# First layers: the convolution's norm in four steps among mLSTM's, K's slabs ahead of the Fourier slabs, and the fills placed anew

## The chip, the core and the metric
One of the cores of a Trainium2 chip runs the whole program. The metric is device microseconds of one execution, the median of several. The five engines run their own instruction streams, in order, and wait for each other on semaphores: PE (TensorE, matrix products into eight PSUM banks), DVE (VectorE), ACT (ScalarE), POOL (GpSimd) and SP (SyncE, here the queue that issues the weight DMAs).

## The reference, cut to what matters
Two blocks run one after the other on 512 tokens of width 1024 (and 256 context tokens in the first block). The first block has two layers. Each does, with modulation vectors that come from `silu(c) @ w_ada` (called ada here):

```
h   = modulate(rmsnorm(x), shift, scale)
z   = h @ w_in                                   # q k v o gates | fourier u | conv a, gate
ym  = mlstm(q, k, v, gates) * sigmoid(o)         # two directions, chunked, q and k through a 3-tap conv
yf  = real(fft over tokens and over 64 channels of u)
yv  = silu(layernorm(dwconv31(a * sigmoid(gate))))
x   = x + gate1 * rmsnorm(concat(ym, yf, yv) @ w_out)
x   = x + gate2 * rmsnorm(relu(modulate(rmsnorm(x)) @ w_mlp1)**2 @ w_mlp2)
```

Layer 0 does this for tokens and context, layer 1 for tokens (its context goes into mLSTM's state only). The second block has two layers with retention, sparse attention and gated linear attention. The change touches it through the shared planner alone.

## The kernel before
A planner in Python (class `Order`) writes one list of steps, and each engine's program walks that list in order and issues what it has to do for each step. So the list's order is the order of every queue. Steps are `mm` (products of a piece), `ev` (the evacuation of its bank), `post` (small products after it), `split` (ScalarE rounds a weight slab to fp32r in WHI, L2164, POOL subtracts to get the rest in RGR, L2575), and named stages: `modSplit`, `conv` (DVE, taps of the 31-tap convolution, L1673), `mPrep` (five steps that prepare mLSTM's gates), mA, mB, mC, mD, mN, mO (mLSTM), `mxSplit`.

Weights stream in the order in which the planner names them, in slabs of up to 512 KB, through a ring of six (`RING = 6`): SP issues slab i when the last product of slab i - 6 is done (L914 to L922), in order. A piece of kind F multiplies a slab of 128 columns with 512 or 256 tokens: three fp32r products for each k (L1011 to L1013). `place` (L398) decides after all else where each unit's `split` step goes: as early as ring and WHI allow, with costs in microseconds.

Side work is woven in: `begin(steps, period)` opens a list, and each `weave(us)` gives it credit that pays for steps. `run` weaves while it issues a piece and then calls `filling`, which adds a piece's time to `credit`; when this reaches `period` the next ada of `fills` goes in (`fill`, `filling`, `ada`). An ada is two slabs of 512 KB, 16 narrow products (L960), a row copy on ScalarE (L2230), four small products (L1141, L1142) and one small addition on DVE (L1514). `rest(side)` issues what is left of mLSTM's list with one ada after every second step, and `filled` issues the adas that then remain, one behind the other.

`first_layer` (L508) goes: norm and eight modSplits; the conv's `cu` products, the first two side by side (`abreast`); gates; `glu`; `u`; the end of mPrep; the Fourier stage, dftA (L1064) and dftB (L1079) for each token region, with slabs dftc and dfts; then K, v, Q and og products; then the convolution's layernorm (lnA, L1088/L1089, sums and squares; lnB, L1094/L1095, then on ScalarE a Sqrt, on DVE a reciprocal L1685 and two multiplications L1689, on ScalarE Silu L2292); then the mxSplits, the rest of mLSTM and the `w_out` products. `ahead` names the slabs of the first two tasks before other steps; until now it serves the first products alone. PE waits with a piece until the earlier content of its PSUM bank is evacuated; these products turn over the banks 0, 1, 6 and 7.

Of the kernel before, what the change touches and what calls it, by code (L numbers as in the profile page):

```python
# [143 lines left out]
class Order:  # L144
# [54 lines left out]
    def run(self, n, parts, us):  # L199

        for part in parts:
            self.step("mm", n, part)
            self.early()
            self.weave(us / len(parts))
        for m in self.after:
            self.step("post", m)
        self.after = []
        self.step("ev", n)
        self.filling(us)
# [128 lines left out]
    def products(self, jobs, banks=(0, 1), together=0):  # L338
# [54 lines left out]
    def place(self):  # L393
# [114 lines left out]
def first_layer(o, l):  # L508
# [10 lines left out]
    cu = [F(2320, 256, "cu", "evacV", go)]  # L519
    if l == 0:  # L520
        cu = o.ahead(cu)
        o.step("gains", l, (0,))
    else:
        o.laid = [(1, j, "w_ada", 1) for j in range(44, 48, 2)]
        o.step("gains", l, (0,))
        cu = o.norms("o0b", tag, cu)
# [5 lines left out]
    else:  # L532
        o.fill(10.0, (2, range(0, 24, 2), "ada_w_2", 0), (3, range(8, 20, 2), "ada_w_2", 1))
    o.products(cu, (0, 1, 6, 7), 2)
    o.gates(l, tag, (0, 1, 6, 7))
    prep = o.begin([("mPrep", l, i) for i in range(5)], 5.0, -6.0)
    o.products([F(2576, 256, "glu", "evacA", go)], (0, 1, 6, 7))
    conv = o.begin([("conv", l, j, t0, tn, k0) for j in range(2) for t0, tn, _ in oregs for k0 in range(0, 31, 4)], 3.6 if l == 0 else 5.0)
    o.products([F(2064, 256, "u", None, go)], (0, 1, 6, 7))
    o.end(prep)  # L540
    for t0, tn, _ in oregs:
        n = tn // 128
        for ti in range(n):
            for j in range(2):
# [12 lines left out]
    o.products([F(512, 512, "qk", "evacV", GB, dst="K"), T(1024, 512, "v", None, at=[[2, 3, 4], [5, 2, 3]]), F(0, 512, "qk", "evacV", go, dst="Q")],  # L557
               (0, 1, 6, 7))
# [94 lines left out]
def schedule():  # L653
# [7 lines left out]
    o.adas(0, (8,), "w_ada", 0)  # L661
    o.step("rstd", "x0a")
    o.adas(0, (10, 12, 14), "w_ada", 0)
    o.flush()
    for l in range(2):
        first_layer(o, l)
# [39 lines left out]
def design(nc, dram):  # L706
# [779 lines left out]
    def vector(e):  # L1486
# [174 lines left out]
        def conv(l, j, t0, tn, k0):  # L1661
# [4 lines left out]
            for k in range(k0, min(31, k0 + 4)):  # L1666
# [14 lines left out]
        def lnB(p, n):  # L1681
            l, t0, tn = p["l"], p["t0"], p["tn"]
            rs = LNRS[:, 0:tn]
            e.wait_ge(*at("evacA", n))
            e.reciprocal(rs, rs).then_inc(*up("evacV"))  # L1685
            e.wait_ge(*now("evacV"))
            for i in range(2):
                x = MX[:, 6 + i, t0:t0 + tn]
                e.scalar_tensor_tensor(out=x, in0=x, scalar=vec("g_conv_ln", l)[:, i:i + 1], in1=rs, op0=MUL, op1=MUL).then_inc(  # L1689
                    *up("evacV", ("ln", l, i, t0)))  # L1690
# [61 lines left out]
        evacs = {"cu": cu, "glu": glu, "qk": qk, "v": v, "u": u, "ab": ab, "four": four, "lnA": lnA, "lnB": lnB, "out": out,  # L1752
# [368 lines left out]
        def gNorm(l, h):  # L2121
# [7 lines left out]
                  "position": position, "table": table, "ret": ret, "rSq": rSq, "rRoot": rRoot, "rNorm": rNorm, "idx": idx, "top": top, "head": head, "gSums": gSums,  # L2129
# [5 lines left out]
    def scalar(e):  # L2135
# [149 lines left out]
        def lnB(p, n):  # L2285
            l, t0, tn = p["l"], p["t0"], p["tn"]
            e.wait_ge(*at("matmuls", n))
            e.activation(LNRS[:, 0:tn], bank(p), ACT.Sqrt, scale=1.0 / 256, bias=eps).then_inc(*up("evacA", n))
            for i in range(2):
                x = MX[:, 6 + i, t0:t0 + tn]  # L2290
                e.wait_ge(*at("evacV", ("ln", l, i, t0)))
                e.activation(x, x, ACT.Silu, bias=vec("b_conv_ln", l)[:, i:i + 1]).then_inc(*up("evacA", ("conv out", l, i, t0)))  # L2292
# [267 lines left out]
        stages = {"start": start, "split": split, "xsum": xsum, "rstd": rstd, "residual": residual, "modSplit": modSplit, "ev": ev, "post": post,  # L2560
# [163 lines left out]
```

## Time and profile before
| | |
|---|---|
| three runs | 3358.75, 3350.33, 3354.8 us, median 3354.8 |
| profiled execution | 3353.06 us, span 3351.3 us |
| PE busy | 3051.1 us, 91% |
| DVE, ACT, POOL busy | 1417.9, 1009.1, 1046.3 us |
| weight slabs | 504 DMAs of 512 KB, 3.5 us from issue to landing |

The profiled execution is one run with its instructions recorded, and its span runs from the first to the last of them; all positions below are microseconds from that start. Layer 0's mixer lies from about 44 to 560, layer 1's from about 1176 to 1580. Busy time of PE says that a product was in flight. The granted clock (PEclk) is a mean over a stretch: 1.00 is 2.4 GHz, 0.50 is 1.2 GHz. A wait is put down to the instruction that ended it.

### The profile page before, as it was taken

What the parts mean: (1) busy time and instruction counts of PE and PEld (TensorE: products, weight loads), DVE (VectorE), ACT (ScalarE), POOL (GpSimd) and SP (SyncE); (2) the same over time, 40 slices, a digit from 0 to 9 for tenths busy, and PEclk for the clock granted to TensorE, in tenths of its full rate; (3) what the DMA queues carried; (4) which work ended last, traced back from release to release, by engine and by line L of the source; (5) the groups of instructions that cost most, each with busy time, mean ns of one, the idle gap of its engine ahead of it and who ended that gap; (6) DMA issues with size and microseconds to landing.
All of it is one profiled execution on the core that took longest, in us unless ns stands there. A gap on an engine that the chain in (4) does not pass through costs nothing.

```text
span 3351.3 us, 41178 instructions
## 1 busy us (share of the span) xinstructions
PE 3051.1 (91%) x16748; PEld 2452.1 (73%) x16748; DVE 1417.9 (42%) x2601; ACT 1009.1 (30%) x1640; POOL 1046.3 (31%) x508
## 2 busy tenths in 40 slices
PE   6899779899999979967999998999889989998898
PEld 4688568788888857756777776777667767776676
DVE  4584442513324256243521134644472246534822
ACT  3213432312213231333332232233423322334232
POOL 1121114222222412214244442232245423332455
PEclk9999878999999889978899989999999889999999
DMA  5332341111111123321222222122112222121121
GB/s 201 120 113 106 114 164 58 57 63 64 63 63 63 53 82 113 120 95 63 92 94 95 92 67 80 60 69 65 60 56 78 77 70 70 63 64 63 57 70 69
DMA packets 77708, 275.39 MB, mean 82 GB/s; under 512 B 8512, under 2 KB 10304, under 8 KB 77392
## 3 DMA queue, kind: packets, MB, share of 16 engines
q1 hardware_dynamic: 75824, 268.91, 23.8%
q10 hardware_dynamic: 1696, 3.84, 0.3%
q8 instruction: 134, 2.20, 0.3%
q14 instruction: 54, 0.44, 0.0%
HBM read 270.62 MB, written 2.10 MB: 81 GB/s over the span
## 4 chain that ended last, share of the span: by engine, by line
PE 78%; DVE 12%; ACT 4%; issue 3%; POOL 2%; DMA 1%; SPq 0%; DVEq 0%; ACTq 0%; POOLq 0%
PE pb L1011 19%; PE pb L1013 18%; PE pb L1012 18%; PE pb L1121 2%; PE pb L1033 2%; PE pb L1035 2%; PE pb L1034 2%; PE pb L960 2%; POOL RGR L2575 1%; PE pb L1051 1%; PE pb L1052 1%; PE pb L1053 1%; PE pb L1079 1%; DMA RG<-in_W_dram 1%; DVE AR L2071 1%
## 5 line engine op out<-in xcount | busy, mean ns | idle before, releaser
L2575 POOL TENSOR_TENSOR RGR<-RG,WHI 128x1024 fp32r<-128x1024 f32 x354 | 864.4, 2442 | 1861.0 <-ACT WHI L2164 1860.7
L2164 ACT ACTIVATE WHI<-RG 128x1024 fp32r<-128x1024 f32 x354 | 370.5, 1047 | 387.0 <-PE pb L1013 288.3
L1011 PE MATMUL pb<-HI,WHI 128*128 128x512 f32 (+1 forms) x880 | 376.9, 428 | 25.1 <-POOL RGR L2575 7.8
L1013 PE MATMUL pb<-LO,WHI 128*128 128x512 f32 (+1 forms) x880 | 354.5, 403 | 0.0
L1012 PE MATMUL pb<-HI,RGR 128*128 128x512 f32 (+1 forms) x880 | 354.4, 403 | 0.0
L1011 PE MATMUL pb<-HR,WHI 128*128 128x512 f32 (+1 forms) x768 | 278.9, 363 | 16.8 <-POOL RGR L2575 10.1
L1013 PE MATMUL pb<-HR,WHI 128*128 128x512 f32 (+1 forms) x768 | 277.7, 362 | 0.0
L1012 PE MATMUL pb<-HR,RGR 128*128 128x512 f32 (+1 forms) x768 | 277.5, 361 | 0.0
L1013 PE MATMUL pb<-HIDR,WHI 128*128 128x512 f32 (+1 forms) x768 | 274.8, 358 | 0.0
L1011 PE MATMUL pb<-HIDR,WHI 128*128 128x512 f32 (+1 forms) x768 | 273.8, 356 | 1.1 <-ACT RLT L2310 0.8
L1012 PE MATMUL pb<-HIDR,RGR 128*128 128x512 f32 (+1 forms) x768 | 274.2, 357 | 0.0
L1011 PEld LDWEIGHTS pb<-HI,WHI 128*128 128x128 f32 (+1 forms) x880 | 168.4, 191 | 93.2 <-issue 42.0
L1706 DVE TENSOR_TENSOR RLT<-RLT 128x256 f32<-128x256 f32 (+1 forms) x96 | 117.5, 1224 | 206.5 <-ACT RLT L2310 206.3
L1013 PEld LDWEIGHTS pb<-LO,WHI 128*128 128x128 f32 (+1 forms) x880 | 167.8, 191 | 44.5 <-issue 1.6
L1011 PE MATMUL pb<-HH,WHI 128*128 128x512 f32 (+1 forms) x464 | 173.2, 373 | 29.7 <-POOL RGR L2575 18.9
L1012 PEld LDWEIGHTS pb<-HI,RGR 128*128 128x128 f32 (+1 forms) x880 | 168.4, 191 | 39.2 <-issue 5.4
L1011 PEld LDWEIGHTS pb<-HR,WHI 128*128 128x128 f32 x768 | 146.9, 191 | 47.2 <-issue 24.3
L1012 PE MATMUL pb<-HH,RGR 128*128 128x512 f32 (+1 forms) x464 | 166.1, 358 | 0.0
L1013 PE MATMUL pb<-HL,WHI 128*128 128x512 f32 (+1 forms) x464 | 166.1, 358 | 0.0
L1013 PEld LDWEIGHTS pb<-HR,WHI 128*128 128x128 f32 x768 | 147.0, 191 | 23.0
L1012 PEld LDWEIGHTS pb<-HR,RGR 128*128 128x128 f32 x768 | 147.1, 191 | 22.5
L1011 PEld LDWEIGHTS pb<-HIDR,WHI 128*128 128x128 f32 x768 | 144.2, 188 | 26.4 <-issue 2.5
(407 smaller groups left out, 5622.3 us busy)
## 6 DMA issues: line engine op xcount, KB each, us to landing
RG<-in_W_dram SPq DMA_DIRECT2D x504, 512.0 KB, 3.5
XCX<-in_xT_dram ACTq DMA_DIRECT2D x4, 512.0 KB, 12.2
out_dram<-XCX SPq DMA_DIRECT2D x8, 256.0 KB, 2.1
CS<-in_CST_dram ACTq DMA_DIRECT2D x1, 1027.0 KB, 4.9
XCC<-in_ctxT_dram SPq DMA_DIRECT2D x4, 256.0 KB, 13.9
CS<-in_CST_dram SPq DMA_DIRECT2D x1, 523.0 KB, 4.8
RG<-in_W_dram SPq DMA_DIRECT2D x2, 256.0 KB, 2.9
RG<-in_W_dram SPq DMA_DIRECT2D x2, 128.0 KB, 3.4
```

The costliest lines, as they stand in the source:

```text
L960: i = e.matmul(PB[p["banks"][0]][32 * g:32 * g + 32, 0:256], CV[:, :, 4 * h + g], wt[:, g, :], start=h == 0, stop=h == 1, tile_position=(0 ...
L1011: e.matmul(out, hi[:, k, :], xh, start=k == order[0], stop=False)
L1012: e.matmul(out, lo[:, k, :], xh, start=False, stop=False)
L1013: i = e.matmul(out, hi[:, k, :], xl, start=False, stop=k == order[7])
L1033: e.matmul(out, xh[:, sl], hi[:, k, :], start=h == 0 and i0 % per == 0 and k == 0, stop=False)
L1034: e.matmul(out, xh[:, sl], lo[:, k, :], start=False, stop=False)
L1035: i = e.matmul(out, xl[:, sl], hi[:, k, :], start=False, stop=p["final"] and ends and k == nk - 1)
L1051: e.matmul(out, hi[:, k, :], xh, start=k == 0, stop=False)
L1121: m = e.matmul(sum_at(tag, c), squares_at(tag, i)[:, a:a + 128], ones[:, 0:1], start=k == 0 and c == first, stop=k == 7 and c == 5)
L1706: e.tensor_tensor(r, r, r, MUL).then_inc(*up("evacV", ("hidden", i)))
L2164: e.activation(WHI[:, u % 2, 0:n], RG[:, s % RING, 0:n], ACT.Copy).then_inc(*up("weightsA", u))
L2575: e.tensor_tensor(RGR[:, s % RING, 0:n], RG[:, s % RING, 0:n], WHI[:, u % 2, 0:n].bitcast(F32), SUB).then_inc(*up("weightsG", u))
```

## The change
The norm's last part leaves the evacuation of lnB and becomes four steps `lnOut`: two half reciprocals, then one multiplication each, the fourth with both Silus. mLSTM steps are woven between lnA and lnB and ahead of each lnOut. The convolution goes in steps of two taps with a pace by width. K's first two slabs are named before the dft slabs of the tokens (`ahead`), the preparation of the gates is taken out of the weaving during the Fourier stage and put back after it, and the credit for fills is set so that none falls into dftB and the next comes later. The period of layer 1's fills is 24 in place of 10. `rest` spreads the adas by their number. The first products' slabs come before the last two adas of the start, and `place` no longer moves a split past a modSplit. `run` issues posts earlier where more than one waits.

```diff
@@ class Order
+            while len(self.after) > 1:
+                self.step("post", self.after.pop(0))
             self.weave(us / len(parts))
@@ def rest(self, side)
+        every = max(1.5, len(side["steps"]) / max(1, len(self.fills)))
+        due = every
         for i, what in enumerate(side["steps"]):
             self.step(*what)
-            if i % 2 and self.fills:
+            if i + 1 >= due and self.fills:
+                due += every
@@ def products(self, jobs, banks, together, abreast=True)
-            if i < together:
+            if i < together and not abreast:
+                made = max(made, together)
+            elif i < together:
@@ def place(self)
-                while at + 1 < first[u] and begin[at + 1] < begin[free + 1] + 5.5 and begin[at + 1] < begin[first[u]] - 3.6:
+                while at + 1 < first[u] and begin[at + 1] < begin[free + 1] + 5.5 and begin[at + 1] < begin[first[u]] - 3.6 and self.steps[
+                        at + 1][0] != "modSplit":
@@ def first_layer(o, l, cu)
-        o.fill(10.0, (2, range(0, 24, 2), "ada_w_2", 0), (3, range(8, 20, 2), "ada_w_2", 1))
+        o.fill(24.0, (2, range(0, 24, 2), "ada_w_2", 0), (3, range(8, 20, 2), "ada_w_2", 1))
...
-    conv = o.begin([("conv", l, j, t0, tn, k0) for j in range(2) for t0, tn, _ in oregs for k0 in range(0, 31, 4)], 3.6 if l == 0 else 5.0)
+    paces = [2.4 if tn == 512 else 1.3 for j in range(2) for t0, tn, _ in oregs for k0 in range(0, 31, 2)]
+    conv = o.begin([("conv", l, j, t0, tn, k0) for j in range(2) for t0, tn, _ in oregs for k0 in range(0, 31, 2)], paces)
     o.products([F(2064, 256, "u", None, go)], (0, 1, 6, 7))
-    o.end(prep)
+    keys = None
+    o.beside.remove(prep)
...
+        if t0 == NC:
+            keys = o.ahead([F(512, 512, "qk", "evacV", GB, dst="K")])
+            o.credit = -1.0e6
...
-    o.products([F(512, 512, "qk", "evacV", GB, dst="K"), T(1024, 512, "v", None, at=[[2, 3, 4], [5, 2, 3]]), F(0, 512, "qk", "evacV", go, dst="Q")],
-               (0, 1, 6, 7))
+    o.credit = -17.0
+    o.beside.append(prep)
+    o.products(keys, (0, 1, 6, 7), 2, False)
+    o.end(prep)
+    o.products([T(1024, 512, "v", None, at=[[2, 3, 4], [5, 2, 3]]), F(0, 512, "qk", "evacV", go, dst="Q")], (0, 1, 6, 7))
...
     for t0, tn, _ in oregs:
         o.run(o.piece("lnA", [], [o.bank()], ["evacV"], l=l, t0=t0, tn=tn, how="lnA"), [ALL8], 1.7)
+        o.weave(3.0)
         o.run(o.piece("lnB", [], [o.bank()], ["evacA"], l=l, t0=t0, tn=tn, how="lnB"), [ALL8], 1.7)
+        for i in range(4):
+            o.weave(1.5)
+            o.step("lnOut", l, t0, tn, i)
+    o.weave(1.5)
@@ def schedule()
-    o.adas(0, (8,), "w_ada", 0)
+    o.adas(0, (8, 10), "w_ada", 0)
     o.step("rstd", "x0a")
-    o.adas(0, (10, 12, 14), "w_ada", 0)
+    cu = o.ahead(first_products(0))
+    o.adas(0, (12, 14), "w_ada", 0)
@@ vector
-        def lnB(p, n):
...
+        def lnOut(l, t0, tn, i):
+            h = tn // 2
+            if i == 0:
+                e.wait_ge(*at("evacA", ("ln root", l, t0)))
+            if i < 2:
+                rs = LNRS[:, i * h:i * h + h]
+                e.reciprocal(rs, rs).then_inc(*up("convV", ("ln factors", l, t0, i)))
+                return
+            x = MX[:, 4 + i, t0:t0 + tn]
+            for k in range(2):
+                e.wait_ge(*at("convV", ("ln factors", l, t0, k)))
+            e.scalar_tensor_tensor(out=x, in0=x, scalar=vec("g_conv_ln", l)[:, i - 2:i - 1], in1=LNRS[:, 0:tn], op0=MUL, op1=MUL).then_inc(
+                *up("evacV", ("ln", l, i - 2, t0)))
@@ scalar
+        def lnOut(l, t0, tn, i):
+            if i == 3:
+                for i in range(2):
+                    x = MX[:, 6 + i, t0:t0 + tn]
+                    e.wait_ge(*at("evacV", ("ln", l, i, t0)))
+                    e.activation(x, x, ACT.Silu, bias=vec("b_conv_ln", l)[:, i:i + 1]).then_inc(*up("evacA", ("conv out", l, i, t0)))
```

## Rows read from the trace of the kernel before

**Rows 1.** The page: the span, and PE's busy time (share of the span) and instructions.
```profile
span 3351.3 us, 41178 instructions
PE 3051.1 (91%) x16748; PEld 2452.1 (73%) x16748; DVE 1417.9 (42%) x2601; ACT 1009.1 (30%) x1640; POOL 1046.3 (31%) x508
```

**Rows 2.** Busy time by stretch: PE, PEld, DVE, ACT, POOL, granted clock, DMA share, GB/s.
```profile
155.00:161.00 6.00, 6.00 (x29) 5.92 (x29) 0.16 (x1) 0.20 (x1) 0.00 (x0) 0.54 0.33 135
161.00:177.00 16.00, 10.97 (x65) 8.35 (x64) 15.27 (x16) 3.71 (x6) 5.23 (x2) 0.91 0.10 33
177.00:262.00 85.00, 85.00 (x636) 75.41 (x635) 70.41 (x101) 16.77 (x26) 20.18 (x8) 1.00 0.36 124
...
357.00:393.00 36.00, 18.69 (x79) 12.80 (x80) 15.44 (x31) 13.77 (x25) 1.85 (x2) 0.66 0.14 53
...
426.00:479.00 53.00, 36.55 (x265) 27.59 (x267) 26.17 (x113) 20.09 (x45) 3.45 (x3) 0.73 0.40 146
479.00:489.00 10.00, 9.23 (x65) 5.40 (x58) 1.73 (x9) 3.67 (x6) 4.71 (x4) 0.50 0.70 244
1240.00:1249.00 9.00, 1.10 (x3) 0.89 (x4) 8.07 (x33) 0.51 (x2) 0.00 (x0) 0.64 0.34 130
...
1277.00:1318.00 41.00, 40.93 (x255) 35.18 (x254) 32.60 (x45) 10.28 (x15) 9.79 (x5) 0.96 0.24 83
1318.00:1430.00 112.00, 107.95 (x759) 91.60 (x758) 38.75 (x72) 28.83 (x46) 26.59 (x11) 1.00 0.40 137
1426.00:1451.00 25.00, 16.90 (x104) 12.00 (x103) 10.41 (x18) 12.02 (x23) 2.06 (x2) 0.93 0.36 132
...
1477.00:1529.00 52.00, 24.45 (x132) 21.95 (x130) 26.16 (x108) 17.65 (x37) 3.67 (x3) 0.71 0.04 17
```

**Rows 3.** Timeline, layer 0's first modSplits: start, us, engine, line, operation, [idle before <-releaser].
```profile
46.42 1.14 DVE L1601 SCALAR_TENSOR_TENSOR HL<-AR,MOD,HH 128x256 fp32r<-128x256 f32 x2
...
48.36 4.87 POOL L2575 TENSOR_TENSOR RGR<-RG,WHI 128x1024 fp32r<-128x1024 f32 x2 [47.91 <-ACT WHI L2164]
...
48.78 4.99 DVE L1601 SCALAR_TENSOR_TENSOR HL<-AR,MOD,HH 128x256 fp32r<-128x256 f32 x2
...
50.92 0.55 PE L1011 MATMUL pb<-HH,WHI 128*128 128x256 f32 x1 [7.50 <-POOL RGR L2575]
```

**Rows 4.** Chain of waits behind dftB, layer 0, then layer 1: start, us, what.
```profile
147.21 3.53 DMA RG<-in_W_dram
...
151.96 2.35 POOL RGR L2575
...
1268.83 3.94 DMA RG<-in_W_dram
```

**Rows 5.** Chain between layer 1's u and dftA.
```profile
1241.72 0.60 DVE AR L1650
...
1248.27 5.90 PE pb L1064 x16
```

**Rows 6.** Chain at K's evacuations, layer 0: a tap beside POOL, and one alone.
```profile
163.00 2.79 DVE AR L1673
...
166.60 0.76 DVE AR L1673
```

**Rows 7.** Timeline, the norm of layer 0.
```profile
386.47 3.35 DVE L1685 RECIPROCAL AR<-AR 128x512 f32<-128x512 f32 x1 [2.70 <-ACT AR L2288]
...
392.37 2.07 PE L1234 MATMUL pb<-CS 64*128 64x128 f32 x8 [7.81 <-DVE AR L1878]
```

**Rows 8.** Chain, an ada in a full stretch and what follows it.
```profile
409.50 1.03 PE pb L960 x16
...
411.07 1.00 PE pb L1255 x8
```

**Rows 9.** Timeline of ACT, a table load and the activation behind it.
```profile
355.12 1.28 ACT L2277 ACT_TABLE_LOAD   x1
356.42 0.60 ACT L2277 ACTIVATE AR<-pb 128x512 f32<-128x512 f32 x1
```

More of the change, by code:

```diff
@@ L336, in gates, with products @@
         self.after.append(p)
-    def products(self, jobs, banks=(0, 1), together=0):
+    def products(self, jobs, banks=(0, 1), together=0, abreast=True):
         tasks = jobs if together else self.tasks(jobs)
@@ L505, in norm_stages, with first_products, first_layer @@
     return [(x + "Sq", l, h) for h in range(5)] + [(x + "Root", l)] + [(x + "Norm", l, h) for h in range(4)]
-def first_layer(o, l):
+def first_products(l):
+    return [("F", "w_in", l, 0, 2320, 256, "cu", "evacV", {"groups": GB if l == 0 else GX, "x": "H1", "tag": f"x{l}a"})]
+def first_layer(o, l, cu):
     go = GB if l == 0 else GX
@@ L517, in T @@
         return ("T", "w_in", l, 0, c0, n, how, by, {"tiles": range(6), "x": "H1", "tag": tag, **more})
-    cu = [F(2320, 256, "cu", "evacV", go)]
     if l == 0:
-        cu = o.ahead(cu)
         o.step("gains", l, (0,))
@@ L525, in first_layer @@
         o.step("gains", l, (0,))
-        cu = o.norms("o0b", tag, cu)
+        cu = o.norms("o0b", tag, first_products(l))
     for k in range(8):
@@ L660, in schedule @@
     o.step("xsums")
-    o.adas(0, (8,), "w_ada", 0)
+    o.adas(0, (8, 10), "w_ada", 0)
     o.step("rstd", "x0a")
-    o.adas(0, (10, 12, 14), "w_ada", 0)
+    cu = o.ahead(first_products(0))
+    o.adas(0, (12, 14), "w_ada", 0)
     o.flush()
     for l in range(2):
-        first_layer(o, l)
+        first_layer(o, l, cu)
     for l in range(2):
@@ L1665, in conv @@
                 e.wait_ge(*at("evacV", ("glu", o.last["glu", l, "evacA", None])))
-            for k in range(k0, min(31, k0 + 4)):
+            for k in range(k0, min(31, k0 + 2)):
                 f = off31[t0] - 15 + k
@@ L1679, in lnA @@
                 e.scalar_tensor_tensor(out=x, in0=bank(p), scalar=-1.0 / 256, in1=x, op0=MUL, op1=ADD).then_inc(*up("evacV", n))
-        def lnB(p, n):
[L1682 to L1690, printed above, removed]
+        def lnOut(l, t0, tn, i):
[11 more added lines that the diff above has]
+                *up("evacV", ("ln", l, i - 2, t0)))
         def out(p, n):
@@ L1750, in gateY @@
                 e.tensor_tensor(y, y, SGT[j], ADD).then_inc(*up("evacV", ("sum", l, n2, j)))
-        evacs = {"cu": cu, "glu": glu, "qk": qk, "v": v, "u": u, "ab": ab, "four": four, "lnA": lnA, "lnB": lnB, "out": out,
+        evacs = {"cu": cu, "glu": glu, "qk": qk, "v": v, "u": u, "ab": ab, "four": four, "lnA": lnA, "out": out,
                  "out2": out2, "relu2": relu2, "plus": plus, "v2": v2, "cp": cp, "silu2": silu2, "gateY": gateY}
@@ L2128, in vector @@
                   "modSplit": modSplit, "pads": pads, "conv": conv, "mPrep": mPrep, "mA": mA, "mB": mB, "mC": mC, "mD": mD, "mN": mN, "mO": mO,
-                  "position": position, "table": table, "ret": ret, "rSq": rSq, "rRoot": rRoot, "rNorm": rNorm, "idx": idx, "top": top, "head": head, "gSums": gSums,
+                  "lnOut": lnOut, "position": position, "table": table, "ret": ret, "rSq": rSq, "rRoot": rRoot, "rNorm": rNorm, "idx": idx, "top": top, "head": head, "gSums": gSums,
                   "gStart": gStart, "gLevel": gLevel, "gOut": gOut, "gState": gState, "gSq": gSq, "gRoot": gRoot, "gNorm": gNorm}
@@ L2287, in lnB @@
             e.wait_ge(*at("matmuls", n))
[L2288 to L2292, printed above, removed]
+            e.activation(LNRS[:, 0:tn], bank(p), ACT.Sqrt, scale=1.0 / 256, bias=eps).then_inc(*up("evacA", n, ("ln root", l, t0)))
+        def lnOut(l, t0, tn, i):
[4 more added lines that the diff above has]
+                    e.activation(x, x, ACT.Silu, bias=vec("b_conv_ln", l)[:, i:i + 1]).then_inc(*up("evacA", ("conv out", l, i, t0)))
         def out(p, n):
@@ L2558, in gRoot @@
             e.activation(GRS, PB[3][:, 384:400], ACT.Sqrt, scale=1.0 / 128, bias=eps).then_inc(*up("glaA", ("root", l)))
-        stages = {"start": start, "split": split, "xsum": xsum, "rstd": rstd, "residual": residual, "modSplit": modSplit, "ev": ev, "post": post,
+        stages = {"lnOut": lnOut, "start": start, "split": split, "xsum": xsum, "rstd": rstd, "residual": residual, "modSplit": modSplit, "ev": ev, "post": post,
                   "mPrep": mPrep, "mA": mA, "mB": mB, "mN": mN, "mO": mO, "mxSplit": mxSplit, "position": position, "table": table, "ret": ret, "rSq": rSq,
```

## The prediction, before the result
> **What bounds the kernel now.** I read the page first: TensorE is busy for 91% of a span of 3351.3 us [rows 1], and the chain that ends last is mostly TensorE. Nothing is to be won inside its products; what an edit of order can win is the remaining 300 us of idle time, the half-rate time behind each pause, and work that can move from a full stretch into a pause. Then the table by stage [rows 2]: in it PE busy against the length of the stretch is what to see. The projections run full (177 to 262: 85.0 of 85), and beside them stand pauses: 5.0 us in 161 to 177, 17.3 in 357 to 393 (the convolution's norm of layer 0), 16.5 in 426 to 479 (mLSTM), 7.9 in 1240 to 1249, 8.1 in 1426 to 1451 (the norm of layer 1) and 27.6 in 1477 to 1529 (mLSTM). Last I took the chain of waits in each pause, to see who ends it [rows 3 to 7].
>
> **The start.** The two weight splits of the first products are issued behind the second modSplit. POOL does both from 48.36 to 53.23, and VectorE's two operations that begin at 48.78 take 4.99 us where the pair before them took 1.14; the first product starts at 50.92 behind POOL [rows 3]. After the change these slabs are loaded ahead of the last two adas, and no split is moved past a modSplit, so both splits run before VectorE begins its modSplits. VectorE gets back 3.85 us; ScalarE now does two splits (1.2 each at most, the gap between the DMA's end and POOL's start in [rows 4]) ahead of the last ada's row copy, of which some 0.7 puts off the gains. Net 3 us (bounds: 0, if the slabs land late, and 5). VectorE and PE are nearly level in the eight modSplits, so not more. The Trainium skill (SBUF — State Buffer, section "SBUF: two separate sides") says that a VectorE operation with two SBUF inputs and a GpSimd operation that reads SBUF take one shared port as an exclusive lock. By that rule the trace agrees, and it would be blocked for at most one POOL split, 2.4 us, each time the two meet. That speaks against the change in one place: K's first two splits now meet the convolution's taps in the Fourier stage instead of an idle VectorE.
>
> **K's slabs before the Fourier slabs.** K's first slab needs ring places that the four dft slabs hold until their last product. The chain shows it: DMA from 147.21, split, POOL until 154.31, 7.1 us; in layer 1 from 1268.83, DMA 3.94, then the same ScalarE and POOL work (3.5), 7.4 us [rows 4]. With both slabs ahead of dft's and split during it, PE goes straight on: 7.1 + 7.4 = 14.5 us. What is late next: the four dft slabs then hang on the last u products and one ada, and their stage begins some 6 us of small products later, so they land in time; K's third slab hangs on K's first task, 8.4 us ahead of use against the 7.1 of the same path. Bounds 10 and 14.5. Behind each pause PE runs at the low level: 155 to 161 is granted 0.54 [rows 2], and six microseconds at half rate do three microseconds' work. That is 2 to 3 us in both layers each, and 1.7 in layer 1's small products after 1248. Of some 6 I take 4 (bounds 0 and 6).
>
> **Gates' preparation.** In layer 1 its steps 3 and 4 stand between u and the Fourier products. VectorE ends u's copy at 1242.32 and PE starts dftA at 1248.27 [rows 5]: 5.95 us. The copy itself stands behind four taps of the convolution; with two taps a step it comes 1.5 us sooner. 7.4 off. The steps now fall into K's first pieces. PE reaches step 4 some 5 us of work after step 3, VectorE needs the same 5.6 us for step 3's small operations plus a K evacuation and a tap step in front of them, so PE will stand at step 4 for about 3 us, and ScalarE, which waits inside step 3, holds K's copies meanwhile. Net 4.4 (bounds +1 lost, if all of it comes back in K, and 7.4). In layer 0 the five steps were already spent during u, nothing changes there.
>
> **Convolution in steps of two taps.** Layer 0 before: 32 steps at 3.6, 115 us of weaving. After: 32 at 1.3 and 32 at 2.4, 118.4; layer 1: 16 x 5.0 = 80 becomes 32 x 2.4 = 77. So the density stays and only the lumps go. In 161 to 177 PE loses 5.0 us [rows 2], since K's evacuation stands behind eight taps at 0.76, two of which took 2.8 to 2.9 us beside POOL [rows 6]. I take 3 of these 5 (bounds 0 and 5). VectorE has the room: 70.4 of 85 us and 32.6 of 41 [rows 2].
>
> **Fills (adas) in other places.** One ada inside a full stretch costs PE 1.57 us (409.50 to 411.07) [rows 8]. Counting credits: layer 0 had 9 adas between dftB and og, one of them free inside the 7.1 us pause; now K's credit of -17 leaves 7. One paid less: 1.6. Layer 1, period 24 instead of 10: 9 before og (one free), now 3; five paid less: 7.9. Where do they go? Into mLSTM's last steps, and there is a direct comparison: the same 17 steps (from mN of chunk 4) take 426 to 479 in layer 0 with eight adas and 1477 to 1529 in layer 1 with none, 53 against 52 us [rows 2]. Eight adas cost 1 us there. So layer 1's rest pays 2 for nine of them, and 2.5 for the eleventh, which stands behind the last step.
>
> **The norm among mLSTM's steps.** Layer 0: 34.5 of the 36 us from 357 to 393, from lnA to the last mO, with 4 mLSTM steps and 17.3 us of PE idle; the longest, 7.81, ends with the mLSTM gating that stands behind a reciprocal of 3.35 [rows 2, 7]. Now 17 steps stand in it (12.4 + 12.4 + 1.5 us of weaving at 1.5). The 13 extra ones took 33.6 us (392.4 to 426) with 6 to 7 adas (10 us). Now they stand in the pauses: 34.5 + 33.6 - 10 = 58, less two thirds of the pauses, about 12: 46 us. 17 steps are left for the rest with 19 adas; `every` becomes 1.5, which places 11, and 8 run serially behind the last step with the one that falls on it. Before, three such adas took the 10 us from 479 to 489 [rows 2], 3.1 each; nine take 25 at 2.8, since the clock rises while they run. Sum: 46 + 56 (the 53, and three adas more than now) + 25 = 127 against 34.5 + 33.6 + 53 + 10 = 131: 4 gained. Bounds: 17 gained (all pauses filled, tail 20) and 7 lost (none filled, 28). Layer 1: 25 us (1426 to 1451) with 3 steps become some 30 with 10; the 7 steps leave the rest, with some 12 us (the 26 from 1451 to 1477 hold ten steps, four adas and a stop for w_out's slab, which stays); nine adas and the last one cost the 4.5 above: 12 - 5 - 4.5, about 3 gained, with bounds 12 gained and 6 lost.
> The split norm alternates ScalarE's tables more: I count two loads more in layer 0 and one in layer 1, and a load takes 1.28 us with the next activation 0.02 behind it [rows 9]: 3.9 us, taken into the 46 and the 30. The Trainium skill (ScalarE: Activation LUTs, section "What ACT_TABLE_LOAD costs") puts a switch at 1.28 plus a drain of 1.38; by that these loads would be 8 us, 4 more, but these rows show no such gap.
>
> **Nothing.** Earlier posts of turned rows (`after` longer than one) move small products by one piece within full stretches: 0, within 1 either way. The second layers' planning is otherwise as before.
>
> **The sum.** 3 + 14.5 + 4 + 4.4 + 3 + 1.6 + 7.9 + 4 + 3 = 45.4 us. The profiled execution took 3353.1 us, 1.8 more than its span; that gives 3307.7. The median of the runs is 3354.8, 1.7 more than it: 3309.
>
> **Rivals.** (a) VectorE becomes the bound in K. For: in layer 1 it gets 7 us of preparation more while PE loses adas, 32.6 + 7 of about 36, and taps can be blocked by POOL. Against: four banks let PE run some 12 us ahead, and v after K needs VectorE little (38.8 us of VectorE work in the 112 from 1318 [rows 2]). It would eat 10 to 14 us, both layers together: 3321. (b) The order of the norm costs rather than pays: reciprocals, squares and Silu stand in front of mLSTM's own operations on its serial chain, and the nine adas at the end show: 7 + 6 lost in place of 4 + 3 gained, 20 us: 3329. For it: the chain there passes through all three queues in turn. Against: VectorE 15.4 and ScalarE 13.8 busy of 36. (c) The pauses fill wholly and the clock stays up: 17 + 12 in place of 7, plus 2: 3285. (d) It doesn't do what it says: the planner still puts K's splits behind dftB, so the 14.5 and the 4 aren't won: 3328. (e) Slower: VectorE falls behind from K's first piece, and each of the 16 K pieces waits for a tap step and a blocked tap, 1.5 + 2.1 = 3.6 us: 58 lost, 3367. It decides from a backlog on VectorE of more than four banks, 12 us, at K's start. In the Fourier stage nothing new comes to VectorE but two blocked taps, so little speaks for it.
>
> **Chances.** Forecast (3299 to 3317) 0.52; (a) 0.18; (b) 0.11; (c) 0.08; (d) 0.05; (e) 0.03; no change within 0.3% (10 us, what a measurement of this kernel can tell from none) 0.03. Range 3287 to 3333, which leaves out the ends of (c), (b), and (e). Faster 0.94, same 0.03, slower 0.03.
>
> **What would show it.** Right: PE busy through what is now 147 to 161 and 1269 to 1277; dftA in layer 1 some 7 us after u's last product at most 3; first product near 47.5; two K splits on POOL during dftB; a row of nine adas before w_out in layer 0; no stretch of 50 us without adas in layer 1's mLSTM. Wrong: PE waiting for VectorE's K evacuations for more than 5 us a layer; the norm stages longer than 52 and 36 us; dftB waiting for a slab.

## The result and the profile after

Four runs of the changed kernel: 3332.69 to 3338.41 us, median 3337.3, against 3354.9 for the kernel before beside it: ratio 0.9945, 95% interval 0.9928 to 0.9963, 18 us faster where 45 were forecast. A second series (e13) gave 0.9931 (0.9917 to 0.9944). Weighted by their intervals the two make 0.9936 within 0.0011, 21 us; the experiments are read against that.

The page of the changed kernel, beside [rows 1]: PE is busy for 16 us more in a span that is 15 us shorter.

```profile
span 3335.9 us, 41190 instructions
PE 3067.3 (92%) x16748; PEld 2463.5 (74%) x16748; DVE 1421.9 (43%) x2604; ACT 1013.0 (30%) x1643; POOL 1046.0 (31%) x508
```

The projections' products come in the same order in all these traces, so the same product can be looked up in each. Length of the stages, from one such product to another, in us ("Q, first half" is its first two slabs of four):

| stage | before | changed | changed (e13) |
|---|---|---|---|
| layer 0: start to glu | 75.1 | 78.7 | 75.5 |
| glu to K | 79.3 | 74.4 | 74.5 |
| K and v | 87.4 | 81.5 | 79.5 |
| Q, first half | 19.1 | 24.2 | 24.2 |
| Q's second half and og | 89.0 | 89.1 | 88.8 |
| norm, mLSTM, adas, to w_out | 140.1 | 155.6 | 148.4 |
| w_out and MLP | 653.8 | 654.0 | 653.7 |
| layer 1: norm to K | 133.9 | 113.2 | 114.0 |
| K to w_out | 251.2 | 252.4 | 250.5 |
| all behind, to the last product of the second block | 1804.6 | 1795.0 | 1789.2 |

Layer 1's mixer is 20 us shorter (forecast: some 25). Layer 0's, forecast some 20 shorter, is 13 and 1 longer. And what lies behind, forecast 0, gained 10 to 15. The two profiles of one plan differ by 7 us in the mLSTM row alone, so single profiles say nothing below that there.

The windows of that row, each cut at the same product: before (the last steps; the adas behind them), then the changed kernel, then e13 (norm; the last steps; the adas). The last steps are 17, an `mN`, which has no product, and 16 more:

```profile
423.30:478.50 55.20, 38.75 (x277) 29.83 (x277) 28.38 (x120) 21.19 (x46) 2.95 (x3) 0.75 0.43 154
478.50:488.80 10.30, 9.53 (x66) 5.48 (x65) 1.85 (x9) 3.67 (x6) 5.01 (x4) 0.50 0.67 231
```
```profile
355.50:402.70 47.20, 34.06 (x210) 28.57 (x210) 25.75 (x63) 22.77 (x44) 2.52 (x2) 0.88 0.09 35
402.70:473.00 70.30, 52.80 (x336) 39.51 (x335) 32.74 (x121) 26.64 (x60) 10.90 (x11) 0.65 0.41 150
473.00:502.10 29.10, 26.83 (x185) 14.66 (x184) 2.78 (x15) 5.98 (x12) 4.93 (x4) 0.50 0.83 297
```
```profile
350.50:399.10 48.60, 35.90 (x207) 29.97 (x206) 25.73 (x63) 22.86 (x44) 2.52 (x2) 0.82 0.09 33
399.10:460.60 61.50, 42.09 (x336) 32.54 (x335) 32.35 (x121) 26.30 (x60) 10.90 (x11) 0.80 0.47 171
460.60:489.70 29.10, 26.80 (x186) 14.61 (x185) 2.81 (x15) 5.96 (x12) 4.78 (x4) 0.50 0.82 300
```

The norm takes 47 and 49 us, 46 were forecast. The last steps took 55.2 us before, with seven adas among them; they take 70.3 and 61.5 with ten. PE waits in them for the row copy or the addition of an ada, but hardly more than before: it idles 17.5 and 19.4 us, against 16.5. What differs is PE's own time. Multiplied by the granted clock it is 34 us in both profiles (52.8 x 0.65, 42.1 x 0.80), and 29 before (38.75 x 0.75): three adas more are some 5 us of work at the full clock, and the rest is the clock. The 9 us between the two profiles, with the same products, come with the clock: PE's own time differs by 10.7. Why it is granted differently, no run shows.

Two of these waits in the changed kernel, then the row of adas, first, second and last of nine, 3.14 us from one to the next:

```profile
414.94 0.38 PE L1165 MATMUL pb<-CS,WT 128*128 128x2 f32 x2 [4.01 <-ACT WT L2258]
423.57 1.10 PE L984 MATMUL pb<-RG,CV 128*32 128x256 f32 x16 [2.44 <-DVE MOD L1538]
472.97 1.95 PE L984 MATMUL pb<-RG,CV 128*32 128x256 f32 x16
476.12 1.94 PE L984 MATMUL pb<-RG,CV 128*32 128x256 f32 x16 [0.25 <-DVE MOD L1538]
...
498.12 1.95 PE L984 MATMUL pb<-RG,CV 128*32 128x256 f32 x16 [0.25 <-DVE MOD L1538]
```

K's first product, at 153.09, follows dftB at once (before: 7.3 us later). But PE stops in K and in Q. The chain at the first stop, and the timeline's POOL and PE rows:

```profile
179.79 0.50 DVE AR L1697
...
180.84 2.67 DVE AR L1697
...
184.71 0.76 DVE AR L1657
...
185.51 1.10 PE pb L984 x16
```
```profile
180.86 2.35 POOL L2606 TENSOR_TENSOR RGR<-RG,WHI 128x1024 fp32r<-128x1024 f32 x1 [2.82 <-ACT WHI L2192]
...
185.51 1.10 PE L984 MATMUL pb<-RG,CV 128*32 128x256 f32 x16 [3.77 <-DVE AR L1657]
249.98 1.10 PE L984 MATMUL pb<-RG,CV 128*32 128x256 f32 x16 [3.46 <-DVE AR L1657]
```

A tap of 0.50 us takes 2.67 while POOL splits, the K evacuation stands behind it, and PE waits for that evacuation before an ada. The first of the two stops is not wholly new: before, PE waited 5.03 us ahead of its first ada in K, which is the 5.0 us of idle time between 161 and 177 in [rows 2]. The stop in Q is new.

```profile
174.16 1.94 PE L960 MATMUL pb<-RG,CV 128*32 128x256 f32 x16 [5.03 <-DVE AR L1633]
```

In layer 1 PE stops twice within K, for the gates' preparation and for K's third slab:

```profile
1281.64 0.27 PE L1238 MATMUL pb<-CS 64*128 64x64 f32 x1 [1.09 <-DVE CS L1822]
...
1286.54 0.26 ACT L2422 ACTIVATE CS<-CS 128x64 f32<-128x64 f32 x1 [3.82 <-DVE CS L1831]
1287.75 1.05 ACT L2192 ACTIVATE WHI<-RG 128x1024 fp32r<-128x1024 f32 x1
...
1291.68 0.36 PE L1035 MATMUL pb<-HH,WHI 128*128 128x256 f32 x1 [2.56 <-POOL RGR L2606]
```

The third slab was requested at 1279.17 and had landed at 1282.65, but ScalarE, in order, waited for VectorE inside the preparation until 1286.54 and split it only at 1287.75.

The gain that was not forecast, in the second block: timeline before, then changed, at the rotary products of its first layer.

```profile
2029.43 1.13 PE L1175 MATMUL pb<-AR,CS 128*128 128x512 f32 x2 [1.51 <-DVE AR L1533]
...
2031.15 2.34 POOL L2575 TENSOR_TENSOR RGR<-RG,WHI 128x1024 fp32r<-128x1024 f32 x1 [11.12 <-ACT WHI L2164]
2031.32 2.72 DVE L1533 TENSOR_TENSOR AR<-AR 128x512 f32<-128x512 f32 x1
...
2034.16 0.62 PE L1011 MATMUL pb<-HI,WHI 128*20 128x512 f32 x1 [3.27 <-DVE MOD L1514]
```
```profile
2022.49 1.13 PE L1199 MATMUL pb<-AR,CS 128*128 128x512 f32 x2 [1.51 <-DVE AR L1557]
...
2027.71 0.41 PE L1035 MATMUL pb<-HI,WHI 128*20 128x512 f32 x1 [0.25 <-DVE MOD L1538]
```

Before, VectorE's turn of the two pieces (and an addition blocked by a POOL split, 2.72 for 0.69) stood between two pieces' products; after, 15 products stand over it, and 3.27 us of waiting become 0.25.

### The profile page after: what moved, and what is told of

Read it like the earlier page. It is cut to its first block, busy times and chain, and to the rows that moved or that the text cites. A ratio compares the mean times of both kernels' runs of the same rounds, so it can differ in the third digit from the quotient of the medians.

```text
span 3335.9 us, 41190 instructions
## 1 busy us (share of the span) xinstructions
PE 3067.3 (92%) x16748; PEld 2463.5 (74%) x16748; DVE 1421.9 (43%) x2604; ACT 1013.0 (30%) x1643; POOL 1046.0 (31%) x508
## 4 chain that ended last, share of the span: by engine, by line
PE 79%; DVE 12%; ACT 4%; issue 3%; POOL 1%; DMA 1%; SPq 0%; DVEq 0%; ACTq 0%; POOLq 0%
PE pb L1035 18%; PE pb L1037 18%; PE pb L1036 18%; PE pb L1145 2%; PE pb L984 2%; PE pb L1057 2%; PE pb L1059 2%; PE pb L1058 2%; PE pb L1075 1%; DVE AR L1697 1%; PE pb L1076 1%; PE pb L1077 1%; PE pb L1103 1%; DVE AR L2099 1%; POOL RGR L2606 1%
## 5 line engine op out<-in xcount | busy, mean ns | idle before, releaser
L1036 PEld LDWEIGHTS pb<-HR,RGR 128*128 128x128 f32 x768 | 147.1, 191 | 22.6
## 6 DMA issues: line engine op xcount, KB each, us to landing
XCC<-in_ctxT_dram SPq DMA_DIRECT2D x4, 256.0 KB, 13.9
```

The lines of the kernel that those rows point to most:

```text
L1036: e.matmul(out, lo[:, k, :], xh, start=False, stop=False)
```

## Experiments

Differences are in us against the changed kernel (0.9936), or against before for e1, e9 and e14, from the ratios and their 95% intervals.

**e1, the posts alone.**
```diff
@@ before: def run
+            while len(self.after) > 1:
+                self.step("post", self.after.pop(0))
```


> The kernel before with one edit of the change, the two lines in run that issue the turned rows' products (posts) as soon as two of them wait. In the plan this moves exactly two pairs of posts, one pair in each layer of the second block, ahead of 15 of the 24 products they stood behind. Theory A (where the gain of the change comes from): the trace after shows the lead over before grow by 6.4 us near 2025 to 2040 and by 7.5 near 2704 to 2726, so this edit alone takes 13.9 us off: 3341 us. Rival B (what I predicted for it): 0 within 1, 3355 us, and the gain seen there belongs to something else.


Measured: 0.9979 (0.9970 to 0.9987), 7 us faster than before (4 to 10). In its trace the lead over before grows at the two places. My 13.9 left out that PE's first wait for VectorE comes earlier too (2.0 and 3.6 us lost just ahead): net of it the trace of e1 has 4.7 and 7.2, the changed kernel's 4.8 and 7.2. Theory A, at half to nine tenths of its size.

**e2, the start as before; e13, the changed kernel again.**
```diff
@@ changed: def schedule
-    o.adas(0, (8, 10), "w_ada", 0)
+    o.adas(0, (8,), "w_ada", 0)
     o.step("rstd", "x0a")
+    o.adas(0, (10, 12, 14), "w_ada", 0)
+    o.flush()
     cu = o.ahead(first_products(0))
-    o.adas(0, (12, 14), "w_ada", 0)
-    o.flush()
@@ def place
-  and self.steps[at + 1][0] != "modSplit"
```


> The changed kernel with its start as before: the first two weight slabs named after the last ada, their splits among the modSplits. Theory A: naming them first costs the last two adas 3.9 us of DMA time (the start is bound by the weight stream) and the slabs of gates and glu come later too; the changed kernel enters glu 3.5 us later than before did where 3 us earlier was forecast, so undoing the start gives 3.5 back, and up to 6 if the pause at the end of u shrinks with it (the lag is 5.7 us at the first Fourier product): 3332 to 3334 us. Rival B (my prediction): the start is worth 3 us, undoing it gives 3340 us.

> The changed kernel itself once more, beside the others and with more runs, since effects of 3 to 6 us are read against it and its ratio so far rests on four runs. Theory A: the spread of the start (glu begins at 75.1 to 78.7 us in eight profiles of one plan) and of the clock in layer 0's mLSTM stage is most of the difference between its copies; ratio to before 0.993 to 0.996. If it comes out below 0.993, the 5 us that e2 showed for the start were this spread.


Measured: e2 0.9930 (0.9917 to 0.9944), e13 0.9931: the start is worth nothing that can be told, 2 within 6, and the runs alone decide between neither view of e2. The traces help: glu begins at 75.1 to 78.7 us in the nine profiles with the early slabs and at 74.6 to 79.8 in the eight without them, so no gain shows. PE's timeline in e13:

```profile
48.35 0.55 PE L1035 MATMUL pb<-HH,WHI 128*128 128x256 f32 x1 [3.87 <-DVE HL L1625]
69.48 0.64 PE L1131 MATMUL pb<-HH,RG 128*32 128x256 f32 x8 [1.30 <-DMA RG<-in_W_dram]
75.52 0.36 PE L1035 MATMUL pb<-HH,WHI 128*128 128x256 f32 x1 [0.67 <-POOL RGR L2606]
```
The first product does come 2.6 us sooner than in [rows 3], but then PE waits for the gates' slab and for glu's split, where before it waited for neither. The slabs named early are numbers 12 and 13 now; the gates' slab is 18 and needs the place of 12, which is in use until the last cu product.

**e3, adas inside layer 0's norm.**
```diff
@@ changed: def first_layer
             o.step("lnOut", l, t0, tn, i)
+            if l == 0 and o.fills:
+                before, o.soon = o.soon, []
+                o.ada(*o.fills.pop(0))
+                for m in before:
+                    o.step("post", m)
```


> The changed kernel with one ada behind each of the eight lnOut steps of layer 0, so that none is left for the end of mLSTM. Theory A: the ten adas in a row before w_out cost 3.14 us each at the low clock, 29 us, and the norm's stage has some 16 us of PE idle time and DMA engines 15% busy; moved there, eight adas cost 1 to 1.6 us each, and the clock rises: 15 to 20 us faster, 3317 to 3322 us. Rival B: the stage is bound by the serial chain through VectorE and ScalarE, and each ada's row copy and addition lengthen it by 2 to 3 us: within 5 us of the changed kernel, 3332 to 3337 us.


Measured: 0.9877 (0.9862 to 0.9892), 20 us faster (within 6): theory A. The windows of its norm and of what follows, to w_out:

```profile
353.00:411.50 58.50, 50.04 (x366) 37.93 (x365) 27.28 (x70) 25.57 (x52) 2.53 (x2) 0.82 0.44 162
411.50:478.40 66.90, 45.32 (x360) 33.22 (x359) 34.30 (x130) 29.50 (x64) 15.31 (x13) 0.77 0.48 172
```
Eight adas lengthen the norm from 47.2 and 48.6 to 58.5 us, 1.3 each; at the end they had cost 3.14 each.

**e4, no mLSTM steps inside the norm.**
```diff
@@ changed: def first_layer
-        o.weave(3.0)
...
-            o.weave(1.5)
...
-    o.weave(1.5)
```


> The changed kernel without the weaving of mLSTM steps inside the norm, in both layers; the norm's four steps follow each other, and 13 more steps (7 in layer 1) are left for the rest with its adas. Theory A: in layer 0 weaving saved only 3.4 us between the norm's start and the last mLSTM step, and lost 19 in the row of adas behind it; with 30 steps left all 19 adas find a place, so layer 0 gets some 19 us shorter (the 134.3 us of the kernel before, less two or three of the adas in its tail), layer 1 within 3 us: 3318 to 3325 us. Rival B (my prediction's reasoning): the weaving fills pauses of 12 us in layer 0 and 12 in layer 1, and the row of adas costs 15: then undoing it costs 10 to 15 us, 3347 us or more.


Measured: 0.9886 (0.9872 to 0.9900), 17 us faster (within 6): theory A. From the last og product to w_out layer 0 takes 137.8 us, against 155.6 and 148.4 with the weaving and 140.1 before; layer 1 from K to w_out 251.6, as with it.

e3 and e4 together separate the weaving from the adas. Layer 0's stretch from the last og product to `w_out`, split where the last steps begin, with the number of adas in each part (counted to `w_out`'s first product, 1.5 us less than in the table above):

| | before | changed | e13 | e14 | e3 | e4 |
|---|---|---|---|---|---|---|
| norm and the steps ahead of the last 17 | 73.2 (8) | 54.7 (1) | 56.4 (1) | 56.3 (1) | 66.1 (9) | 72.6 (9) |
| last steps and the adas behind | 65.5 (10) | 99.5 (19) | 90.5 (19) | 90.4 (17) | 66.9 (11) | 63.7 (11) |

With nine adas in the first part and eleven in the second in both, the weaving (e3 against e4) saves 6.5 us in the first and gives back 3.2 in the second: 3 us by the traces, 3 within 7 by the runs. What it loses in the changed kernel is the adas that no longer find room beside it.

**e14, the norm in four steps alone, added to before** (with the weaving and `rest` as changed).


> The kernel before with the part of the change that gives it its name, alone: the norm in four steps among mLSTM's in both layers, with the new spacing of the adas in rest; everything else as before. The plan differs from before's only there. Theory A: in layer 0 17 adas meet 17 steps, 11 find a place and 7 stand in a row at the end at 3.14 us each against 3 before (+12.6), the middle gets 3 to 4 us shorter; layer 1 has five adas and no such row, 0 within 2: 8 to 10 us slower than before. Rival B (my prediction's terms, 4 and 3, with three adas fewer to place): 7 us or more faster.


Measured: 1.0035 (1.0022 to 1.0047), 12 us slower than before (7 to 16): theory A. The part that names the change costs, with the adas placed as they are. Its tail, seven adas in the window, then w_out:

```profile
474.00:497.00 23.00, 21.22 (x146) 11.60 (x145) 2.49 (x13) 5.20 (x10) 5.10 (x4) 0.50 0.81 290
```
Four adas more than before (12.6 us). The stretch ahead of them, to the last mO, is 4.4 us shorter than before, with four adas fewer in it. Layer 1, with five adas in both kernels, takes 107.4 us from the last og product to w_out against 106.2: the weaving gives nothing there.

**e5, adas in the rotation of four banks.**
```diff
@@ changed: def ada
-        n = self.piece("ada", slabs, [self.bank()], ["evacV"], i=i, j=j, how="ada")
+        n = self.piece("ada", slabs, [self.bank(self.where)], ["evacV"], i=i, j=j, how="ada")
@@ def first_layer: o.where = (0, 1, 6, 7) ahead of glu, (0, 1) ahead of og
```


> The changed kernel, but from glu to Q each ada takes the next of the four PSUM banks 0, 1, 6, 7 as the products do; now it takes bank 0 or 1 by turns, which can be one that a product took only two pieces earlier. Theory A: the two stops of PE in layer 0 that are new in the changed kernel (3.77 us at 181.75 ahead of an ada in K, 3.46 at 246.52 ahead of an ada in Q, each with some 1.5 us at a lower clock behind it) come from that short reuse, with the evacuation behind taps that run beside a POOL split: 8 to 10 us go. Rival B: VectorE is simply late, and PE stops one piece later for the same time: within 3 us of the changed kernel.


Measured: 0.9908 (0.9890 to 0.9926), 9 us faster (within 7): theory A, and the windows over K's first 29 us and over the first half of Q show both stops gone:

```profile
152.00:181.00 29.00, 29.00 (x170) 25.05 (x169) 25.20 (x36) 6.94 (x10) 5.76 (x3) 1.00 0.34 125
...
228.80:248.10 19.30, 19.30 (x124) 16.19 (x121) 14.56 (x18) 4.31 (x7) 5.24 (x2) 1.00 0.48 164
```

**e6, the convolution in four-tap steps with the old paces.**
```diff
@@ changed
-    conv = o.begin([... for k0 in range(0, 31, 2)], paces)
+    conv = o.begin([... for k0 in range(0, 31, 4)], 3.6 if l == 0 else 5.0)
-            for k in range(k0, min(31, k0 + 2)):
+            for k in range(k0, min(31, k0 + 4)):
```


> The changed kernel with the convolution in steps of four taps and the paces 3.6 and 5.0 of before, all else as changed. My prediction's term: steps of two taps are worth 3 us here (of the 5.0 idle in K) and the copy behind four taps 1.5 us in layer 1, so undoing them costs 3 to 5 us. Theory A, after the traces: the pace of 1.3 for the narrow region puts 22 taps in front of the gates' last preparation instead of 16 and costs 2.1 us at the end of u in layer 0, which comes back, and the stops in K and Q are lumps of VectorE's queue in either form: within 3 us of the changed kernel. Rival B: the stops in K grow to 5 us each: 8 us slower.


Measured: 0.9956 (0.9944 to 0.9968), 7 us slower (within 5): my term, or rival B. In the trace K and v take 85.5 us in place of 81.5 and 79.5, layer 1's way from the gates' stage to dftA 3.5 more; Q gets 2.6 back and the end of u 2.2. The stop in K grows from 3.77 to 6.70 us, as rival B has it:

```profile
185.68 1.94 PE L983 MATMUL pb<-RG,CV 128*32 128x256 f32 x16 [6.70 <-DVE AR L1656]
```

**e7, K's slabs not named early; e9, only the credits of the change, added to before.**
```diff
@@ e7, changed: def first_layer
-            keys = o.ahead([F(512, 512, "qk", "evacV", GB, dst="K")])
...
-    o.products(keys, (0, 1, 6, 7), 2, False)
+    o.products([F(512, 512, "qk", "evacV", GB, dst="K")], (0, 1, 6, 7))
@@ e9, before: def first_layer
+        if t0 == NC:
+            o.credit = -1.0e6
...
+    o.credit = -17.0
```


> The changed kernel without the early naming of K's first two slabs (they are named behind the four Fourier slabs, as before); the credit and the preparation's place stay as changed. Theory A, and my prediction's term: PE stands 7.1 us in layer 0 and 7.4 in layer 1 behind the Fourier stage again and runs some 6 us at half rate behind each, 14.5 + 4: 18 us slower than the changed kernel, less up to 4 because VectorE catches up in the pause and the stops in K get shorter: 14 to 18 us slower. Rival B: the gain was only moved, the stops in K and the late third slab in layer 1 (2.56 us) take back what the early slabs give: 5 to 9 us slower.

> The kernel before with the credit for fills alone set as in the change: -1.0e6 ahead of the tokens' dftB and -17 behind it, in both layers; K's slabs are not named ahead. In the plan no ada stands between dftB and K any more, K's first slab is then number 37 and needs the ring place of slab 31, an ada's, where it was number 39 and needed that of slab 33, a Fourier slab. Theory A, after e7: this alone removes PE's pauses of 7.1 and 7.4 us behind the Fourier stage; one ada less stands in a pause in each layer and comes back in mLSTM for up to 3.1 us: 10 to 14 us faster than before, 3337 to 3341. Rival B: K's early slabs were needed for it (my prediction), and this edit leaves the pauses: within 3 us of before.


Measured: e7 0.9940 (0.9928 to 0.9952), no difference (1 within 5): both views of e7 fall. K still follows dftB at once. Since no ada stands between them, K's first slab is number 37 and needs an ada's old place; naming it early adds nothing to that (naming it early with the ada left in dftB was not run). In layer 1 the stop for the third slab is gone, but PE waits 3.10 us ahead of dftB where it waited 1.14.

e9: 0.9991 (0.9980 to 1.0002), 3 us faster (from 7 faster to 1 slower), with the pause gone in both layers (K begins at 147.38 in layer 0): the mechanism of A, not its gain. The 7 us come back as two adas more in mLSTM (147.1 us from the last og product to w_out against 140.1), and in layer 1 the gates' preparation now meets K's split. Timeline of e9:

```profile
1245.21 4.64 POOL L2578 TENSOR_TENSOR RGR<-RG,WHI 128x1024 fp32r<-128x1024 f32 x2 [15.47 <-ACT WHI L2167]
1245.26 2.32 DVE L1783 TENSOR_TENSOR CS<-CS 128x8 f32<-128x8 f32 x1
1247.61 2.26 DVE L1785 TENSOR_TENSOR CS<-CS 128x8 f32<-128x8 f32 x1
...
1253.54 0.36 PE L1217 MATMUL pb<-CS 64*128 64x64 f32 x1 [12.95 <-DVE CS L1797]
```
Two operations of 0.17 us take 2.3 each, and the pause ahead of dftA is 12.95 where it was 8.71.

**e10, the preparation finished ahead of the Fourier stage.**
```diff
@@ changed: def first_layer
-    o.beside.remove(prep)
+    o.end(prep)
...
-    o.beside.append(prep)
```


> The changed kernel with the gates' preparation finished ahead of the Fourier stage, as before. In layer 0 all its steps are spent by then, so the plan differs in layer 1 alone. Theory A, from the traces: between the last u product and the first Fourier product PE stood 10.5 us before and stands 2.0 beside one ada now; two-tap steps account for some 3 of it (e6), so the preparation's place is worth 5 to 7 and costs 1.1 in K: 4 to 6 us slower than the changed kernel. Rival B: the 5 us come back in K, where the steps are missing from VectorE's queue and the stop of 2.56 us for the third slab has time to vanish: within 2 us.


Measured: 0.9926 (0.9911 to 0.9942), 3 us faster (within 6): A falls, B stands. PE waits again ahead of dftA, and K runs without a stop: the third slab, still named early, lands at 1281.75 and ScalarE splits it at 1281.77. So the stop of 2.56 us needs both: the slab that the ring lets in late (gone in e7) and the preparation's new place, which holds ScalarE (gone here). Below, the timeline's row of the wait, then the window of K and v, and the same of the changed kernel:

```profile
1248.58 0.36 PE L1236 MATMUL pb<-CS 64*128 64x64 f32 x1 [7.52 <-DVE CS L1820]
```
```profile
1270.00:1342.00 72.00, 72.00 (x523) 66.17 (x522) 47.91 (x61) 15.04 (x21) 17.59 (x7) 1.00 0.29 102
```
```profile
1270.60:1348.00 77.40, 73.74 (x521) 67.11 (x520) 54.10 (x92) 16.63 (x28) 16.99 (x7) 0.98 0.27 93
```

**e8, layer 1's fills every 10 us.**
```diff
-        o.fill(24.0,
+        o.fill(10.0,
```


> The changed kernel with a period of 10 in place of 24 for layer 1's fills. In the plan nine adas then stand between the Fourier stage and the norm instead of six, and seven behind the norm instead of eleven. Theory A (my prediction's term by count): three or four more in a full stretch at 1.57 us each, 5 to 6 us, against half a microsecond saved for each in the pauses of mLSTM: 3 to 5 us slower. Rival B: an ada among mLSTM's steps costs as much as in a full stretch, since it stands at the low clock and lengthens the chain: within 2 us.


Measured: 0.9953 (0.9938 to 0.9968), 6 us slower (within 6): theory A's size, though the interval doesn't exclude B. The traces speak for A: from glu to the end of Q, with four adas more, layer 1 takes 157.6 us against 148.9 and 147.9, and from og to w_out, with four fewer, 153.6 against 153.2 and 151.2.

**e11, e12, e15, the findings together.**
```diff
@@ changed, with e2's start, e3's adas, e5's banks
-    paces = [2.4 if tn == 512 else 1.3 ...
+    paces = [2.4 if tn == 512 else 1.8 ...
@@ e12, besides
-            if l == 0 and o.fills:
+            if o.fills:
@@ e15: e11 with e7's edit
```


> The changed kernel with what e2, e3 and e5 tell: the start as before, one ada behind each lnOut of layer 0, each ada in the next of the four banks from glu to Q; and a pace of 1.8 in place of 1.3 for the convolution's narrow steps, which puts 16 to 18 taps instead of 22 in front of the gates' last preparation (2.1 us at the end of u). Theory A: the gains are in different stages and add up: 5 (e2) + 23 (e3) + 12 (e5) + 2 = 42 us below the changed kernel, with 5 off because e5's number holds a lucky part (9 to 10 by its own trace): 3290 to 3298 us. Rival B: they overlap, since what comes earlier meets the same adas and the same low clock in mLSTM: 3305 us or more.

> The kernel of e11 with an ada behind each lnOut in layer 1 too (four of twelve). Theory A: in layer 1 no ada stands behind the last mLSTM step but one, so nothing is saved at the end; they fill the norm's pauses (1.5, 1.8 and 3.1 us) and keep the clock up: 1 to 4 us faster than e11. Rival B: they push VectorE's and ScalarE's steps of the norm back: 2 us slower or more.

> The kernel of e11 without the early naming of K's slabs. Theory A, after e7 and e9: the pauses behind the Fourier stage went with the ada that stood there, so nothing is lost, and in layer 1 the stop of 2.56 us for K's third slab goes: 0 to 4 us faster than e11. Rival B: 3 us or more slower, since K's first splits now come late.


Measured: e11 3301.8 us, 0.9835 (0.9816 to 0.9854): 55 us under before and 34 (within 7) under the changed kernel, between its two theories. e12 0.9866 (0.9849 to 0.9883), 10 slower than e11: B; in layer 1 no adas stand in a row at the end, and from K to w_out it takes 256.5 us against 249.7. e15 0.9857 (0.9844 to 0.9871): 7 slower by the runs (within 8), though its trace is 7 shorter behind the start; not settled, and e11 stands.

## Why the prediction was wrong

The forecast was a sum of nine terms. By place, layer 1 came to 20 of some 25 us, layer 0 failed, and the second block had no term.

- **The norm among mLSTM's steps, layer 0 (4 gained).** The step that failed is "`every` becomes 1.5 ... 46 + 56 + 25". By the same products the three parts are 47 and 49, 70.3 and 61.5, and 29 in both profiles: 8 to 15 us lost in place of 4 gained. The 46 held. The 56 was the 53 from 426 to 479 and one microsecond for each of three more adas; but by then the last steps had begun (423.3, so 55.2), and three adas are some 5 us of PE's work at the full clock, in a stretch that is granted 0.65 and 0.80. The 25 was short because I let the clock rise in the row of adas; it stayed at 0.50. Nor would a faster clock have brought the row down to the 1.57 of a full stretch: the DMA engines are busy for 0.82 of it, by my estimate 2.6 of each 3.14 us. By itself the norm costs 12 us (e14), and the four adas more in the row are 12.6. Of rival (b), its nine adas at the end are shown, at a higher price; that the norm's own operations on the chain cost more than the weaving pays is not (e3 against e4).
- **The norm, layer 1 (3 gained).** Nothing: 107.4 us against 106.2 with the same adas (e14). That the adas behind the norm cost next to nothing there held (e8).
- **Earlier posts (0).** The step is the paragraph "Nothing". I looked at the moved posts where they stand in full stretches and never looked up the two places in the second block, where VectorE's turn stood open between pieces. 7 us by the runs.
- **K ahead (14.5) and the clock (4).** The pauses went as forecast, but the cause named is not the one that did it: no ada behind dftB is enough (e9), and early naming adds nothing to it (e7). The term was read as a gain of the whole; an ada that stands in a pause for nothing goes to the row at 3.14, which gives 7 back in layer 0. In layer 1, where no row exists, norm to K is 20 us shorter, in which the preparation's pause and two adas fewer are counted too.
- **Stops in K and Q (no term of their own).** 3.77 + 3.46 and some 1.5 us of low clock behind each. Rival (a) had the blocked taps and the price, and the convolution's term had the 5.0 us in K, 3 of which it took off; what I missed is that an ada can take a bank used two pieces before (e5), so "four banks let PE run some 12 us ahead" was wrong wherever one does.
- **The start (3).** VectorE's pair of operations went from 4.99 to 1.14 us and the first product came 2.6 sooner in e13 (0.9 later in the first profile); then PE waits 1.30 and 0.67 for the gates' and glu's slabs. I priced only the edit's own two slabs, not the one six numbers behind.
- **K's third slab, layer 1 (2.56, no term).** I had 8.4 us for a path of 7.1. The path took 12.5 us, from the request at 1279.17 to the product at 1291.68, and 5.1 of it is the landed slab waiting for ScalarE. That the preparation holds ScalarE stands in the prediction for K's copies, and not for K's splits.
- **Preparation (4.4).** The pause went from 8.7 to 0.9, and 6.3 came back in K's stops and clock (77.3 against 71.1 us to the same product). Net nothing (e10); I had put 3 for it.
- **Convolution (3, and 1.5 in the preparation's term): 7 (e6). Fills in layer 1 (7.9, less some 4.5): 6 (e8).** Right within their intervals, as were the three table loads. The 1.6 for layer 0's fills went into the row with the rest.

The single edits, added or undone alone, make 12 lost (e14) against 7 + 3 + 7 + 6 gained, 11 in all, and the whole has 21. The difference is no larger than their intervals together, some 11, so a joint part is not shown by the runs. One shows in a trace: without the preparation moved, K's split delays it by 4.2 us (e9). The Trainium skill (SBUF — State Buffer, section "SBUF: two separate sides") states an exclusive lock between a VectorE operation with two SBUF inputs and a GpSimd operation that reads SBUF. By that rule the traces agree in each collision: 0.50 to 2.67, 0.69 to 2.72, 0.17 to 2.32 us beside splits of 2.3. What I did with it was to ask where blocked taps end a wait, and not where a chain of small operations does.

## What to carry to other kernels

Work that fills a pause has a place of its own: before taking it out, ask where it goes and at what clock it runs there, and put it into the pauses that are left before other work takes them. Compare two plans from the same product to the same product, and ask whether a longer stretch waits more or runs at a lower clock. A buffer named early in a ring can move the wait to the request one ring length later. And when a planner's rule changes, list every step it moves, to the end of the program.

## What was not expected of the hardware

A row of nine adas, one behind the other, kept PE busy for 26.8 of 29.1 us (e13), with the DMA engines at 82%, and the granted clock stayed at 0.50 (1.2 GHz) to its end; in the w_out products that follow it is 1.00 from 495 us on. The same plan took 148.4 and 155.6 us from the last og product to w_out in two profiles, with granted clocks of 0.76 and 0.71. Over the eight profiles whose last steps have the same plan and the row of nine behind them, these steps took 61.4 to 70.3 us, with 0.80 to 0.65 granted: the size of several effects studied here.
